# The last convolution: who makes which taps (ScalarE two of 31 for six blocks, VectorE 192 and TensorE 64 tokens of the shared block)

## The chip, the core and the metric

The kernel runs on one NeuronCore of a Trainium2 chip, as one program. The metric is the device time of one execution in microseconds; the median of three runs stands for the kernel. TensorE, VectorE, ScalarE, GpSimd and SyncE each work through their own instructions in the written order and meet at semaphores.

## The reference

The function is a decoder block (gated delta rule with a short convolution, cross attention over a memory, a product-key mixture of experts) followed by two residual mixers over 256 tokens and 1024 channels, all in float32. The change concerns the first of the two, a gated convolution of width 31 along the tokens, one filter for each channel:

```python
def _conv_mixer(h, w_in, dw, db, ln_g, ln_b, w_out):
    a, b, g = jnp.split(h @ w_in, 3, axis=-1)
    y = a * jax.nn.sigmoid(b)
    y = lax.conv_general_dilated(
        y, dw[:, None, :].astype(y.dtype), window_strides=(1,),
        padding=[(CONV_WIDTH_2 // 2, CONV_WIDTH_2 // 2)],
        dimension_numbers=('NWC', 'WIO', 'NWC'),
        feature_group_count=BRANCH) + db
    y = jax.nn.silu(_layernorm(y, ln_g, ln_b)) * jax.nn.silu(g)
    return y @ w_out
```

The second mixer means over windows of 2 to 16 tokens and follows on the result.

## The kernel before, in words

Channels lie on the 128 partitions, in 8 blocks of 128 channels; tokens lie along the free axis. Weights come in units of 1024 x 512 through a ring of three slots, loaded by SyncE.

Most of the time up to 955 us goes to the experts: GpSimd gathers rows, VectorE makes dot products, TensorE adds up weighted rows. The last stage, from about 960 us on, is the two mixers. It is staged in this order on TensorE (function `last_half` makes half a unit, 2 blocks of 256 tokens, 16 products over k of 128x128 by 128x256):

1. `cv_ab0` to `cv_ab3`: eight halves, one for each block k, with `a` of the block in the first 256 columns of a PSUM bank and `b` in the other 256. The halves go round four banks (`last_free`).
2. `cv_g0` and the first half of `cv_g1`: the gate.
3. The convolution of block 7 (256 tokens) and of part of block 6 through diagonal weights: for each tap a 128x128 matrix `tap_diag` with the tap's weights on the diagonal, times the shifted input (line 892).
4. The channel sum "mean" by a matrix of ones over the eight convolved blocks `yc`, in the order 0 to 5, 7, 6 (line 904). It waits for each block by `conv_dve` or `conv_pe`.
5. The second half of `cv_g1`, its first 16 products, then the channel sum "var" of the squares (line 448), then its other 16 products.
6. `cv_out0`, `cv_out1`, and the second mixer.

ScalarE makes `sigmoid(b)` of each block into one of two buffers (`gate_sigmoid(k)`, line 1287, waits for the half on TensorE and for the gated input k-2), and between them the 62 diagonal matrices, 31 for block 7 and then 31 for block 6 (line 1306). The sigmoids 2, 3 and 4 stand in the first loop behind the taps 3, 13 and 23, sigmoid 5 behind that loop, and 6 and 7 in the second loop behind the taps 3 and 13. Then come the Silu of three gate halves (line 1292), which give their banks free, the bias additions of block 7 and of the last 128 tokens of block 6, and the statistics of the layer norm.

VectorE makes the gated input of each block into the padded buffer `ypad` (function `glu`, line 1888, which frees the PSUM bank), and the taps of blocks 0 to 5 on 256 tokens and of block 6 on its first 128 (function `conv_taps`, lines 1900 for tap 0, 1902 for tap 1 and 1905 for the other 29, each multiplying and adding). Even taps gather in `yc`, odd taps in `odd_taps`, and a last addition joins them (line 1908) and posts `conv_dve`. The order is written out: gated input 0, taps 0 to 15 of block 0, gated input 1, taps 16 to 30 of block 0, gated input 2, taps 0 to 15 of block 1 and so on to gated input 7 in the middle of block 3; then blocks 4, 5 and 6 at a stretch. A tap waits for the one two before it, as both write the same buffer.

`go` posts a semaphore and has its own engine wait for it; `post` only posts. In `need(engine, name, n)` the engine waits until the semaphore has reached n.

Of the kernel before, what the change touches and what calls it, by code (L numbers as in the profile page):

```python
# [7 lines left out]
ALU = mybir.AluOpType  # L8
# [3 lines left out]
P = 128  # L12
# [72 lines left out]
for _i, _n in enumerate([f"{u}{g}" for u in ("c", "h", "z") for g in range(4)]):  # L85
    FILLS[1].setdefault(FILL_FROM - 1 + _i, []).append((_n[:-1], int(_n[-1])))
FILLED = [{s + 1: [u for u, g in f if g == 3] for s, f in FILLS[t].items()} for t in range(TT)]

MOD_CHUNKS = 24
# [60 lines left out]
def build(nc, x_t, mem_t, cols_d, c_d, const_d, small_d, keys_d, units_d, grp_d, mod_d, uv_d, out_d, dbg=None):  # L150
    with ExitStack() as ctx:
# [39 lines left out]
        def area(first, n):  # L191
            return arena[:, first:first + n]
# [85 lines left out]
        sgb = blocks(area(2304, 512), 2)  # L278
        odd_taps = area(2816, S)
        tap_diag = [area(a, CV_TAPS * P).rearrange("p (a c) -> p a c", a=CV_TAPS) for a in (M4, 14336)]  # L280
# [154 lines left out]
        def _(pe):  # L435
# [450 lines left out]

            for i, (b, first, n) in enumerate(((7, 0, S), (6, P, P))):
                need(pe, "tap_diag", CV_TAPS * (i + 1))
                need(pe, "glu", b + 1)
                out = tile_begin("ss_m1")[:, 0:n] if i else ps[:, 7, 0:n]  # L890
                for tap in range(CV_TAPS):
                    mm = pe.matmul(out, lhsT=tap_diag[i][:, tap, :], rhs=ypad[:, b, first + tap:first + tap + n],  # L892
                                   start=(tap == 0), stop=(tap == CV_TAPS - 1))
                post(mm, "conv_sums")
# [37 lines left out]
        def _(act):  # L932
            def go(ins, name):
                return did(act, ins, name)
# [367 lines left out]
            gate_sigmoid(0)  # L1302
            gate_sigmoid(1)
            for i, b in enumerate((7, 6)):
                for tap in range(CV_TAPS):
                    post(act.activation(tap_diag[i][:, tap], ident, ACT.Copy, scale=col("cv_dw", 8 * tap + b)), "tap_diag")
                    if tap % 10 == 3 and 2 + 4 * i + tap // 10 < KB:
                        gate_sigmoid(2 + 4 * i + tap // 10)
                if i == 0:
                    gate_sigmoid(5)  # L1310
            for i in range(3):
                gate_silu("cv_g0", i)
            act.wait_ge(sem("conv_sums"), 1)
            go(act.activation(yc[:, 7], ps[:, 7, 0:S], ACT.Identity, bias=col("cv_db", 7)), "conv_pe")
            act.wait_ge(sem("conv_sums"), 2)
            go(act.activation(yc[:, 6, P:S], tile_ps("ss_m1")[:, 0:P], ACT.Identity, bias=col("cv_db", 6)), "conv_pe")
            tile_ready(act, "mean")
# [34 lines left out]
        def _(dve):  # L1352
# [538 lines left out]
            def conv_taps(b, first=0, end=CV_TAPS):  # L1891

                last = counts.get("tap", 0)
                n = P if b == 6 else S
                for tap in range(first, end):
                    w = col("cv_dw", 8 * tap + b)
                    x = ypad[:, b, tap:tap + n]
                    acc = odd_taps[:, 0:n] if tap % 2 else yc[:, b, 0:n]
                    if tap == 0:
                        last = post(V.tensor_scalar(acc, x, w, col("cv_db", b), ALU.mult, ALU.add), "tap")  # L1900
                    elif tap == 1:
                        last = post(V.tensor_scalar(acc, x, w, None, ALU.mult), "tap")
                    else:
                        need(dve, "tap", last - 1)
                        last = post(V.scalar_tensor_tensor(out=acc, in0=x, scalar=w, in1=acc, op0=ALU.mult, op1=ALU.add), "tap")  # L1905
                if end == CV_TAPS:
                    need(dve, "tap", last)
                    go(V.tensor_tensor(yc[:, b, 0:n], yc[:, b, 0:n], odd_taps[:, 0:n], ALU.add), "conv_dve")

# [160 lines left out]
```

## Time and profile before

| | us |
|---|---|
| Median of 3 runs | 1202.87 (1200.65 to 1203.58) |
| The profiled execution | 1203.55 |
| Its span, first to last instruction | 1201.7 |
| TensorE busy | 881.5 (73%) |
| VectorE busy | 814.8 (68%) |
| ScalarE busy | 265.6 (22%) |
| GpSimd busy | 328.3 (27%) |
| Mean granted TensorE clock, of full speed | 0.801 |

Times count from the start of the span. PE is TensorE's matmul and PEld its weight load, DVE VectorE, ACT ScalarE, POOL GpSimd, SP SyncE; L892 is line 892 of the kernel. A float32 matmul of the program stands as two records. A line of the timeline holds instructions of one kind that follow on each other, with their count behind "x"; in square brackets stands the idle time of the engine before them and what ended it. A line of a stretch reads: from:to and length, then for PE, PEld, DVE, ACT and POOL the busy time and, in brackets, how many instructions, then the granted clock (1.00 is 2.4 GHz, 0.50 is 1.2 GHz), the share of the DMA engines, and GB/s; where it is asked for one line of the kernel, only engines that this line uses stand there. Busy shares are means over stages with different limits, so the stretch around the convolution is read by itself.

### The profile page before, as it was taken

The page shows a single profiled execution, that of the slowest core. Times are in us where ns is not written, and L with a number is a line of the kernel's source. Part 1 is how long each engine was busy: PE and PEld are TensorE (multiplying, and loading weights), DVE is VectorE, ACT ScalarE, POOL GpSimd, SP SyncE. Part 2 cuts the span into 40 slices and gives each one's busy share as a digit, 9 for nine tenths or more (in the row PEclk, how much of TensorE's full clock was granted, in tenths as well). Part 3 has the DMA queues.
Part 4 walks back from the last instruction along what each step waited for, and adds up shares of the span by engine and source line. Part 5 has one row for each costly group of instructions (what it writes and reads, how often), then busy time and mean ns, then how long its engine had stood idle before and what let it go on. Part 6 is the DMA issues. An engine that isn't in the chain of part 4 may idle for free.

```text
span 1201.7 us, 17348 instructions
## 1 busy us (share of the span) xinstructions
PE 881.5 (73%) x6784; PEld 668.7 (56%) x6784; DVE 814.8 (68%) x2102; ACT 265.6 (22%) x541; POOL 328.3 (27%) x284
## 2 busy tenths in 40 slices
PE   6999999977786884877344544443445599999998
PEld 6898687865674672754121221211212298878887
DVE  4766546688998767767797687777764779952411
ACT  2511111135222224121021221111102234132100
POOL 0001000242353333534544355454444200000000
PEclk9999899987897896987555655555655599999999
DMA  9987696799999999999999999999999945213330
GB/s 357 395 332 303 232 402 220 308 423 422 388 418 422 411 422 421 420 420 413 420 420 420 402 375 421 420 420 420 420 420 395 371 165 192 96 70 140 106 140 35
DMA packets 51553, 402.49 MB, mean 335 GB/s; under 512 B 5648, under 2 KB 7952, under 8 KB 9104
## 3 DMA queue, kind: packets, MB, share of 16 engines
q0 software_dynamic: 40320, 293.62, 59.8%
q1 hardware_dynamic: 10288, 105.62, 22.1%
q10 hardware_dynamic: 864, 2.16, 0.5%
q8 instruction: 53, 0.87, 0.3%
q14 instruction: 28, 0.23, 0.0%
HBM read 400.32 MB, written 1.05 MB: 334 GB/s over the span
## 4 chain that ended last, share of the span: by engine, by line
PE 22%; DMA 16%; DVE 7%; issue 2%; POOL 2%; ACT 1%; POOLq 0%; DVEq 0%; ACTq 0%
DMA wring<-uv_dram,arena 16%; PE ps L865 15%; PE ps L572 2%; DVE wring L1486 2%; PE ps L892 2%; POOL wring L430 2%; DVE arena L1486 2%; PE ps L559 1%; DVE arena L1513 1%; PE ps L845 1%; PE ps L448 1%; PE ps L923 1%; DVE arena L1427 0%; ACT arena L1331 0%; PE ps L538 0%
## 5 line engine op out<-in xcount | busy, mean ns | idle before, releaser
L430 POOL DMA_INDIRECT arena<-uv_dram,arena x192 | 234.6, 1222 | 339.3 <-PE ps L572 266.8
L572 PE MATMUL ps<-arena 128*32 128x256 f32 x1536 | 160.0, 556 | 220.5 <-DVE arena L1513 220.5
L1486 DVE CUSTOM_DVE_ANT_0 arena<-arena 128x1024 f32<-128x1024 f32 x192 | 231.6, 1224 | 79.5 <-DMA arena<-uv_dram,arena 74.9
L572 PEld LDWEIGHTS ps<-arena 128*32 128x32 f32 x1536 | 52.1, 142 | 309.9 <-DVE arena L1513 261.6
L865 PE MATMUL ps<-xn,wring 128*128 128x256 f32 x608 | 132.0, 379 | 2.4 <-ACT xn L1279 2.4
L865 PEld LDWEIGHTS ps<-xn,wring 128*128 128x128 f32 x608 | 115.4, 190 | 18.3 <-issue 2.7
L1024 ACT ACTIVATE gel<-dots 128x2 f32<-128x2 f32 x128 | 26.0, 203 | 415.2 <-DVE dots L1486 385.6
L484 PEld LDWEIGHTS ps<-xn,wring 128*128 128x128 f32 x896 | 106.2, 198 | 8.5 <-issue 5.9
L484 PE MATMUL ps<-xn,wring 128*128 128x128 f32 x896 | 109.5, 283 | 1.7 <-DVE xn L1527 1.6
L430 POOL DMA_INDIRECT wring<-uv_dram,arena x64 | 80.5, 1258 | 94.5 <-PE ps L572 84.5
L572 PE MATMUL ps<-wring,arena 128*32 128x256 f32 x512 | 52.4, 548 | 69.4 <-DVE arena L1513 69.3
L1486 DVE CUSTOM_DVE_ANT_0 wring<-wring,arena 128x1024 f32<-128x1024 f32 x64 | 77.4, 1223 | 25.0 <-DMA wring<-uv_dram,arena 24.7
L1513 DVE TENSOR_SCALAR arena<-const,gel,arena 128x32 f32<-128x32 f32 x256 | 65.3, 307 | 39.2 <-ACT gel L1024 36.2
L1905 DVE SCALAR_TENSOR_TENSOR arena<-arena,cols 128x256 f32<-128x256 f32 (+1 forms) x203 | 77.4, 460 | 0.6
L572 PEld LDWEIGHTS ps<-wring,arena 128*32 128x32 f32 x512 | 16.8, 140 | 97.6 <-DVE arena L1513 88.8
L484 PE MATMUL ps<-arena,wring 128*128 128x128 f32 x576 | 69.5, 282 | 2.1 <-DVE arena L1739 2.1
L484 PEld LDWEIGHTS ps<-arena,wring 128*128 128x128 f32 x576 | 67.6, 197 | 6.0 <-issue 3.6
L422 POOL DMA_DIRECT2D arena<-mod_dram x24 | 12.9, 539 | 177.8 <-DVE modc L1821 143.6
L1821 DVE CUSTOM_DVE_ANT_0 arena<-arena 128x1024 f32<-128x1024 f32 x48 | 56.8, 1223 | 3.8 <-DMA arena<-mod_dram 1.7
L865 PE MATMUL ps<-arena,wring 128*128 128x256 f32 x256 | 56.8, 382 | 1.6 <-DVE arena L1933 1.6
L865 PEld LDWEIGHTS ps<-arena,wring 128*128 128x128 f32 x256 | 48.1, 190 | 10.2 <-DVE arena L1933 2.6
L512 PE MATMUL ps<-xn,wring 128*128 128x128 f32 x384 | 51.3, 294 | 0.0
(267 smaller groups left out, 1160.3 us busy)
## 6 DMA issues: line engine op xcount, KB each, us to landing
wring<-units_dram SPq DMA_DIRECT2D x46, 2048.0 KB, 11.4
arena<-mod_dram POOLq DMA_DIRECT2D x24, 1024.0 KB, 9.5
arena<-uv_dram,arena POOLq DMA_INDIRECT x192, 13.8
wring<-units_dram SPq DMA_DIRECT2D x2, 1024.0 KB, 8.4
arena<-units_dram SPq DMA_DIRECT2D x1, 2048.0 KB, 8.8
hA<-x_t_dram SPq DMA_DIRECT2D x2, 512.0 KB, 7.1
arena<-mem_t_dram SPq DMA_DIRECT2D x1, 1024.0 KB, 9.8
arena<-keys_dram ACTq DMA_DIRECT2D x2, 512.0 KB, 6.8
```

Of the source, the lines that this page charges most:

```text
L422: pool.dma_start(mod_w[:, i % MOD_BUFFERS].rearrange("p b d -> p (b d)"), mod_d[i]).then_inc(sem(f"mod_in{i % MOD_BUFFERS}"), 16)
L430: pool.indirect_dma_start(ring[b], None, uv_d, bass.IndirectOffsetOnAxis(ap=idx[:, n:n + 1], axis=0)).then_inc(sem(f"row_in{b}"), 16)
L484: mm = pe.matmul(out[:, j * P:(j + 1) * P], lhsT=lhsT, rhs=src[:, k, :], start=(k == 0), stop=(k == KB - 1))
L512: mm = pe.matmul(out[:, g * P:(g + 1) * P], lhsT=w[:, k, g * P:(g + 1) * P], rhs=xn[:, k, tokens(t)], start=(k == 0), stop=(k == KB - 1))
L572: mm = pe.matmul(acc_ps(q)[G * c:G * (c + 1), :], lhsT=diag[:, s % 2, j, :], rhs=ring[b][:, D + 256 * c:D + 256 * (c + 1)], start=(p == 0 ...
L865: mm = pe.matmul(out[:, j * S:(j + 1) * S], lhsT=w[:, k, (2 * i + j) * P:(2 * i + j + 1) * P], rhs=rhs[:, k, :], start=(k == 0), stop=(k = ...
L892: mm = pe.matmul(out, lhsT=tap_diag[i][:, tap, :], rhs=ypad[:, b, first + tap:first + tap + n], start=(tap == 0), stop=(tap == CV_TAPS - 1))
L1024: post(act.activation(gel[:, s % 2], dots[:, s % 2], ACT.Gelu), "gelu")
L1486: post(V.tensor_tensor_reduce(out=ring[b][:, 0:D], in0=ring[b][:, 0:D], in1=x_rep[q % 2], scale=1.0, scalar=0.0, op0=ALU.mult, op1=ALU.add ...
L1513: post(V.tensor_scalar(diag[:, s % 2, j], cst("stack"), gel[:, s % 2, j:j + 1], gate[:, n:n + 1], ALU.mult, ALU.mult), "diag")
L1821: post(V.tensor_tensor_reduce(out=w, in0=w, in1=silu_c, scale=1.0, scalar=0.0, op0=ALU.mult, op1=ALU.add, accum_out=modc[:, m:m + 1]), "mo ...
L1905: last = post(V.scalar_tensor_tensor(out=acc, in0=x, scalar=w, in1=acc, op0=ALU.mult, op1=ALU.add), "tap")
```

## The change

Six edits. A constant `CV_SPLIT` of 192 takes the place of 128 as the number of tokens of block 6 that VectorE makes; TensorE makes the other 64 and ScalarE adds the bias to these. There are two buffers `odd_taps`, for even and odd blocks. ScalarE has a function `first_taps(b)`, which for blocks 1 to 6 makes tap 0 (with the bias) into `yc` and tap 1 into the block's `odd_taps` and then posts `first_taps`. It is called for block 1 behind sigmoid 3 and for block 2 behind sigmoid 4 in the first loop of diagonals, and for blocks 3 to 6 behind the second loop, ahead of the Silus of the gate. From block 3 on it waits until VectorE has finished block b - 2. VectorE leaves out taps 0 and 1 of these blocks and waits for `first_taps` in their place; taps 2 and 3 no longer wait for a tap before them.

```diff
--- before.py
+++ after.py
@@ -85,6 +85,9 @@
 for _i, _n in enumerate([f"{u}{g}" for u in ("c", "h", "z") for g in range(4)]):
     FILLS[1].setdefault(FILL_FROM - 1 + _i, []).append((_n[:-1], int(_n[-1])))
 FILLED = [{s + 1: [u for u, g in f if g == 3] for s, f in FILLS[t].items()} for t in range(TT)]
+
+
+CV_SPLIT = 192
 
 MOD_CHUNKS = 24
 MOD_BUFFERS = 4
@@ -276,7 +279,7 @@
         hB = blocks(area(12288, 2048), KB)
         ypad = area(0, 8 * 286).rearrange("p (b t) -> p b t", b=KB)
         sgb = blocks(area(2304, 512), 2)
-        odd_taps = area(2816, S)
+        odd_taps = [area(2816 + S * i, S) for i in range(2)]
         tap_diag = [area(a, CV_TAPS * P).rearrange("p (a c) -> p a c", a=CV_TAPS) for a in (M4, 14336)]
         yc, gT, ycn = (blocks(area(5120 + 2048 * i, 2048), KB) for i in range(3))
         vpad = area(14336, 8 * 272).rearrange("p (b t) -> p b t", b=KB)
@@ -884,7 +887,7 @@
             last_half("cv_g1", 0, xn)
 
 
-            for i, (b, first, n) in enumerate(((7, 0, S), (6, P, P))):
+            for i, (b, first, n) in enumerate(((7, 0, S), (6, CV_SPLIT, S - CV_SPLIT))):
                 need(pe, "tap_diag", CV_TAPS * (i + 1))
                 need(pe, "glu", b + 1)
                 out = tile_begin("ss_m1")[:, 0:n] if i else ps[:, 7, 0:n]
@@ -1301,19 +1304,33 @@
             go(act.activation(warm[:], cst("one"), ACT.Sigmoid), "warm")
             gate_sigmoid(0)
             gate_sigmoid(1)
+
+            def first_taps(b):
+
+                n = CV_SPLIT if b == 6 else S
+                need(act, "glu", b + 1)
+                if b >= 3:
+                    need(act, "conv_dve", b - 1)
+                act.activation(yc[:, b, 0:n], ypad[:, b, 0:n], ACT.Identity, bias=col("cv_db", b), scale=col("cv_dw", b))
+                go(act.activation(odd_taps[b % 2][:, 0:n], ypad[:, b, 1:1 + n], ACT.Copy, scale=col("cv_dw", 8 + b)), "first_taps")
+
             for i, b in enumerate((7, 6)):
                 for tap in range(CV_TAPS):
                     post(act.activation(tap_diag[i][:, tap], ident, ACT.Copy, scale=col("cv_dw", 8 * tap + b)), "tap_diag")
                     if tap % 10 == 3 and 2 + 4 * i + tap // 10 < KB:
                         gate_sigmoid(2 + 4 * i + tap // 10)
+                        if i == 0 and tap > 3:
+                            first_taps(tap // 10)
                 if i == 0:
                     gate_sigmoid(5)
+            for b in range(3, KB - 1):
+                first_taps(b)
             for i in range(3):
                 gate_silu("cv_g0", i)
             act.wait_ge(sem("conv_sums"), 1)
             go(act.activation(yc[:, 7], ps[:, 7, 0:S], ACT.Identity, bias=col("cv_db", 7)), "conv_pe")
             act.wait_ge(sem("conv_sums"), 2)
-            go(act.activation(yc[:, 6, P:S], tile_ps("ss_m1")[:, 0:P], ACT.Identity, bias=col("cv_db", 6)), "conv_pe")
+            go(act.activation(yc[:, 6, CV_SPLIT:S], tile_ps("ss_m1")[:, 0:S - CV_SPLIT], ACT.Identity, bias=col("cv_db", 6)), "conv_pe")
             tile_ready(act, "mean")
             tile_used_wait(act, act.activation(rms[:, 0], tile_ps("mean")[:, 0:S], ACT.Copy, scale=1.0 / D), "mean")
             signal(act, "mean_sb", 1)
@@ -1891,21 +1908,24 @@
             def conv_taps(b, first=0, end=CV_TAPS):
 
                 last = counts.get("tap", 0)
-                n = P if b == 6 else S
+                n = CV_SPLIT if b == 6 else S
                 for tap in range(first, end):
                     w = col("cv_dw", 8 * tap + b)
                     x = ypad[:, b, tap:tap + n]
-                    acc = odd_taps[:, 0:n] if tap % 2 else yc[:, b, 0:n]
-                    if tap == 0:
+                    acc = odd_taps[b % 2][:, 0:n] if tap % 2 else yc[:, b, 0:n]
+                    if tap < 2 and b:
+                        need(dve, "first_taps", b)
+                    elif tap == 0:
                         last = post(V.tensor_scalar(acc, x, w, col("cv_db", b), ALU.mult, ALU.add), "tap")
                     elif tap == 1:
                         last = post(V.tensor_scalar(acc, x, w, None, ALU.mult), "tap")
                     else:
-                        need(dve, "tap", last - 1)
+                        if b == 0 or tap > 3:
+                            need(dve, "tap", last - 1)
                         last = post(V.scalar_tensor_tensor(out=acc, in0=x, scalar=w, in1=acc, op0=ALU.mult, op1=ALU.add), "tap")
                 if end == CV_TAPS:
                     need(dve, "tap", last)
-                    go(V.tensor_tensor(yc[:, b, 0:n], yc[:, b, 0:n], odd_taps[:, 0:n], ALU.add), "conv_dve")
+                    go(V.tensor_tensor(yc[:, b, 0:n], yc[:, b, 0:n], odd_taps[b % 2][:, 0:n], ALU.add), "conv_dve")
 
 
             go(V.memset(ypad[:, :, 0:15], 0.0))
```

## Rows read from the trace of the kernel before

**Rows 1.** The page: lines of the chain that ended last, shares of span.
```profile
DMA wring<-uv_dram,arena 16%; PE ps L865 15%; PE ps L572 2%; DVE wring L1486 2%; PE ps L892 2%; POOL wring L430 2%; DVE arena L1486 2%; PE ps L559 1%; DVE arena L1513 1%; PE ps L845 1%; PE ps L448 1%; PE ps L923 1%; DVE arena L1427 0%; ACT 
```

**Rows 2.** The chain in order of time from 1000 us: start, length, what.
```profile
1000.00 37.34 PE ps L865 x173
1037.34 20.31 PE ps L892 x124
1057.64 3.46 PE ps L904 x16
1061.10 3.45 PE ps L865 x16
1064.55 3.47 PE ps L448 x16
```

**Rows 3.** Timeline, 982 to 1065 us: start, length, engine, line, operation.
```profile
982.79 0.42 DVE L1888 TENSOR_TENSOR arena<-ps,arena 128x256 f32<-128x256 f32 x1
...
983.96 5.62 DVE L1905 SCALAR_TENSOR_TENSOR arena<-arena,cols 128x256 f32<-128x256 f32 x14
...
989.03 0.38 ACT L1287 ACTIVATE arena<-ps 128x256 f32<-128x256 f32 x1 [3.46 <-PE ps L865]
...
989.50 0.42 DVE L1888 TENSOR_TENSOR arena<-ps,arena 128x256 f32<-128x256 f32 x1
990.06 6.03 DVE L1905 SCALAR_TENSOR_TENSOR arena<-arena,cols 128x256 f32<-128x256 f32 x15
...
996.12 0.43 DVE L1908 TENSOR_TENSOR arena<-arena 128x256 f32<-128x256 f32 x1
...
1016.65 0.38 ACT L1287 ACTIVATE arena<-ps 128x256 f32<-128x256 f32 x1 [3.46 <-PE ps L865]
1017.07 5.07 ACT L1306 ACTIVATE arena<-const,cols 128x128 f32<-128x128 f32 x17
...
1036.84 0.41 DVE L1900 TENSOR_SCALAR arena<-arena,cols 128x256 f32<-128x256 f32 x1
...
1037.43 11.57 DVE L1905 SCALAR_TENSOR_TENSOR arena<-arena,cols 128x256 f32<-128x256 f32 x29
1049.04 0.42 DVE L1908 TENSOR_TENSOR arena<-arena 128x256 f32<-128x256 f32 x1
1049.50 0.34 DVE L1900 TENSOR_SCALAR arena<-arena,cols 128x128 f32<-128x128 f32 x1
...
1049.95 7.70 DVE L1905 SCALAR_TENSOR_TENSOR arena<-arena,cols 128x128 f32<-128x128 f32 x29
...
1057.68 0.29 DVE L1908 TENSOR_TENSOR arena<-arena 128x128 f32<-128x128 f32 x1
...
1062.98 2.19 ACT L1323 ACTIVATE arena<-arena 128x512 f32<-128x512 f32 x4
```

**Rows 4.** Groups by form, ScalarE, from 1000 us: busy us, mean ns.
```profile
L1306 ACT ACTIVATE arena<-const,cols 128x128 f32<-128x128 f32 x31 | 9.4, 387 | 0.1
...
L1331 ACT ACTIVATE arena<-arena,cols 128x256 f32<-128x256 f32 x8 | 4.8, 600 | 0.3
```

**Rows 5.** Stretches, matmuls of line 892, then of line 624: busy, clock.
```profile
1050.90:1057.30 6.40, 6.40 (x60) 6.40 (x59) 1.00 0.00 0
...
18.90:20.40 1.50, 1.50 (x15) 1.50 (x15) 1.00 1.23 415
```

**Rows 6.** Stretches, all engines: busy (count) per engine, TensorE's granted clock.
```profile
919.90:921.90 2.00, 0.00 (x0) 0.00 (x0) 0.00 (x0) 1.96 (x3) 0.00 (x0) 1.00 0.99 414
921.90:924.00 2.10, 0.00 (x0) 0.00 (x0) 0.24 (x2) 1.77 (x3) 0.00 (x0) 0.50 1.02 425
958.60:962.80 4.20, 4.18 (x19) 4.18 (x20) 2.98 (x10) 2.55 (x6) 0.00 (x0) 0.50 1.03 437
962.90:967.50 4.60, 4.60 (x43) 4.60 (x43) 0.00 (x0) 0.00 (x0) 0.00 (x0) 1.00 0.93 395
```

## The prediction

> **What bounds the kernel now.** I read the page's chain of waits first, then the same chain in order of time for the last 200 us, then the timeline of that stretch engine by engine, and last single stretches for the granted clock. The reader is to see in [rows 1] that next to a transfer the largest part of the chain is TensorE at line 865, the projections of the last stage, and in [rows 2] that the last fifth hangs on TensorE: from 1000 us to 1068 us its matmuls follow one another without a hole, first the projections, then the two convolutions through diagonal weights (line 892), the channel sum "mean" (line 904), half of cv_g1 (line 865) and the sum "var" (line 448). But VectorE is hardly behind. [Rows 3] show its taps: from the gated input of block 2 at 982.79 to the last addition of block 6, which ends at 1057.68 + 0.29 = 1057.97, it goes from one instruction to the next with no wait of note. TensorE leaves the second convolution at some 1057.6 and ends "mean" at 1061.10 [rows 2]. Block 6 is its last term: two records at a step of 0.216 (sixteen in 3.46) and the rest of the last one, 0.6 us in all, so its input may come up to 1060.5, while it comes at 1057.97. VectorE has 2.5 us of slack; what moves its end beyond 1060.5 moves the kernel's end.
>
> **ScalarE's taps.** For blocks 1 to 6 the first two taps leave VectorE, where they cost 0.59 us of its time per block (1037.43 less 1036.84) and 0.45 us at 128 tokens (1049.95 less 1049.50) [rows 3]. On ScalarE a 128x256 ACTIVATE with scale and bias from columns takes 0.60 us, and a 128x128 one with scale alone 0.387 [rows 4]. The second one of a pair is 128x256 with scale alone, so between these, and I take 0.49. 17 copies of 128x128 span 5.07 [rows 3], a step of 0.293, so back-to-back ones overlap by 0.09. A pair is 0.60 - 0.09 + 0.49 = 1.00 us. ScalarE is idle for most of this stretch and its own time costs nothing. What counts is when the pair comes, because VectorE now waits for it before its third tap.
>
> ScalarE works in the written order, and two of the pairs stand behind things that come late:
> - Block 1: its pair is behind the sigmoid of block 3, which follows TensorE at 989.03 and takes 0.38 [rows 3]. The pair starts at 989.44, ends at 990.44, VectorE goes on at 990.49. Before, it began tap 2 at 983.96: 6.5 us of wait. Queued behind it on VectorE are the gated input 3 and all other blocks.
> - From there by the steps of [rows 3] (14 taps and on to the gated input 5.54, then 0.56, 15 taps 6.06, an addition 0.46): gated input 3 at 996.0, addition 1002.7, gated input 4 at 1003.1. TensorE's halves come every 6.9 us (four from 989.03 to 1016.65), and the bank of block 3 is next wanted for block 7, after 1009.7: it is free in time.
> - Block 2: its pair is behind the sigmoid of block 4 (989.03 + 6.9 = 995.9), done at 997.3, before VectorE asks. Taps begin at 1003.7; gated input 5 at 1009.2; addition 1015.8; gated input 6 at 1016.3, VectorE ready for block 3 at 1016.9.
> - Block 3: its pair stands behind the whole second loop of diagonals, in which the sigmoid of block 7 follows TensorE at 1016.65 and then 17 diagonal copies run from 1017.07 to 1022.14 [rows 3]. The pair starts at 1022.16 and ends at 1023.16; VectorE begins tap 2 at 1023.2, after 6.3 us of wait. The first wait is swallowed by this one, whose end TensorE sets.
> - Then: gated input 7 at 1028.75 (TensorE's convolution wants it at 1037.3: safe), addition of block 3 at 1035.4, tap 2 of block 4 at 1035.8. The pair of block 4 needs only the end of block 2 and is there. Block 5's waits for the end of block 3 (1035.8) and has all of block 4 as cover; block 6's for the end of block 4, covered by block 5. A full block is 11.61 + 0.46 = 12.07: addition of block 4 at 1047.4, of block 5 at 1059.5, tap 2 of block 6 at 1059.97 (before 1049.95: 10.0 late).
>
> The three Silu evictions of cv_g0 and their table load now stand behind the pair of block 6: from about 1049 to 1052, not spread from 1022 on. Their banks and results are wanted after "var"; the bias addition of block 7 moves to 1052.5 and is wanted at 1060. "Mean" with its wait for VectorE hides both, and without it each microsecond would count. No DMA is moved. The dropped waits before taps 2 and 3 give nothing: taps follow at 0.400 (11.61/29) by their own length.
>
> **64 more tokens on VectorE.** A tap step is 0.400 at 256 tokens and 0.2666 at 128 (1057.68 less 1049.95, by 29) [rows 3]. No row has 192, so 29 taps take between 7.73 and 11.61, and I take the middle, 9.67, as the two are most likely points of one line. The final addition becomes 0.36. Block 6 ends at 1059.97 + 9.67 + 0.36 = 1070.0, against 1057.97: 12.0 late.
>
> **64 fewer tokens on TensorE.** The second convolution makes 62 records of 128 columns (each tap two). 60 of them begin in 6.40 us, 0.107 each, and the weight loads beside them fill the stretch; with weights of the same 128x128 and only 8 columns, line 624 begins 15 in 1.50 us, 0.100 and at the window's edge 0.107, at the same clock [rows 5]. 64 columns lie between 8 and 128, and so the gain between 0 and 0.4 us; if the step went with the columns it would be half of 6.6, 3.3 us. I take 0, by line 624. The convolution ends long before VectorE either way.
> The Trainium skill (TensorE: Matmul & The Clock Gate, Back-to-back issue gap) gives the spacing of an isolated matmul as N/2.4 + 2.5 ns, 29 ns at 64 columns, which makes an estimate of 1.8 us for 62 of them; its section LDWEIGHTS (loading the stationary operand) gives a weight load by its columns alone, P/1.2, 107 ns at 128. By the second nothing is gained, and the trace agrees with it, 0.107. By the first this sum would be the same too, since VectorE comes last, but the rival without a wait would gain.
>
> **What follows on TensorE.** It works off "mean" for blocks 0 to 5 (the last from 1059.9) and 7 and stands idle from some 1060.9 to 1070.05: nine microseconds with nothing that it may do, as the half of cv_g1 stands behind "mean". What the clock does in such a hole: from 919.9 on TensorE does nothing, the grant is still 1.00 up to 921.9 and 0.50 after (1.2 GHz in place of 2.4); and when it took up full work at 958.6, the grant stayed at 0.50 to 962.8 and was 1.00 from 962.9 [rows 6]. I take both: half speed from 1070.05 for 4.2 us, to 1074.25.
> - The two records of block 6 for "mean": 0.43 each, so the half of cv_g1 begins at 1070.9.
> - Of its 16 records 7.8 fit before 1074.25 at 0.43; the other 8.2 at 0.216 take 1.8: end at 1076.0. At full clock the sixteen take 3.45 (1061.10 to 1064.55, [rows 2]).
> - "Var" needs the squares. The first is done at 1062.98 + 0.62 [rows 3], 2.5 after "mean", the last at 1065.2, 4.1 after; so now at 1073.6 to 1075.2, before TensorE asks. It begins at 1076.1 where it did at 1064.5: 11.6 late.
> Behind "var" the order is as it was and so are the waits, up to the output.
>
> **Sum.** +12.0 for VectorE's end, less 2.5 of slack, gives 9.5; plus 2.1 for the clock +11.6. The profiled execution took 1203.55 us, with a span of 1201.7; it becomes 1215.15. It is 0.68 above the median of the runs, 1202.87, so the forecast is **1214.5 us**. The unknown sizes: the taps at 192 tokens plus or minus 1.9 at their ends, the clock from 0 (1212.4) to 5 (1217.4).
>
> **Rivals.**
> - *The clock stays up.* At 919.9 the grant outlived the end of the work by 2 us [rows 6], and a shorter hole would pass. This one is four times that, which speaks against. Then +9.5, 1212.4.
> - *The clock comes back late*, so that "var" runs at half speed too: 3 us more, 1217.5. For it: the grant has been 0.50 where work is thin. Against: here it is dense, as from 958.6 on.
> - *Only block 1 waits,* because ScalarE has the pair of block 3 when VectorE comes. The steps above less the second wait (6.3): VectorE's end is 1063.7, 3.2 after 1060.5, 1206.1. Against it is the written order: the sigmoid that follows 1016.65 and 17 copies stand in front.
> - *No wait decides, the faster side.* If ScalarE is always ahead, VectorE loses 5 x 0.59 + 0.45 and gains 1.94 + 0.07: 1.4 earlier, 1056.6. With the second convolution bound by its weights TensorE leaves it as before and the time is 1202.9. Only if 64 columns take half the step does it reach "mean" 3.3 earlier, at 1054.3, and then the last term ends at 1056.6 + 0.6 = 1057.2, 3.9 earlier, 1199.0. The gain begins where both hold, ScalarE's pair of block 3 before 1017 and a step below 0.107; the order contradicts the first, line 624 the second.
>
> **Numbers.** The forecast 0.72, clock stays 0.14, clock late 0.07, block 1 alone 0.03, no wait at 1202.9 0.02, no wait and half a step 0.02. A difference of 0.3% (3.6 us) is about what a measurement of this kernel can tell. Range 1211.0 to 1217.3: it takes in the clock that stays, with taps somewhat below the middle, and the edge of the late one. Faster 0.02; same 0.03, the 0.02 and some of "block 1 alone"; slower 0.95.
>
> **What would show it.** VectorE idle twice for some 6 us, released by ScalarE, behind 984 and behind 1017; its final addition of block 6 near 1069.6; TensorE's records of the second convolution still at 0.107; its hole of 9 us before 1070, a grant of 0.50 behind it and the half of cv_g1 taking 5.1 in place of 3.45; all from "var" on in the same shape, shifted. I am wrong if VectorE's taps run on over 984 and 1017, or if these holes are there and the end moves by under 8 us.

## The result, and the profile after

The changed kernel takes 1215.92 us in the median of four runs (1212.57 to 1221.73), the kernel before 1202.65 in four: the ratio is 1.0113, with a 95% interval of 1.0086 to 1.0140, slower by 13.3 us. The profiled execution took 1217.19 us with a span of 1215.3.

The timeline of the changed kernel has the lines that answer to [rows 3]: start and length in us, engine, line, operation, in brackets the idle time ahead and what ended it. Lines 1314 and 1315 are ScalarE's pair, 1925 VectorE's taps, 1928 its last addition, 895 and 907 TensorE's convolution and channel sum, 868 the gate (like all projections), 451 the sum of squares. Line numbers are those of each kernel's own file, so they shift between variants. A matmul of the program stands as two records. A gate half is 16 matmuls; "the 16 records of the gate" below are the 8 of them that stand between the channel sum and the sum of squares, and the other 8 follow behind that sum.

```profile
990.32 0.38 ACT L1290 ACTIVATE arena<-ps 128x256 f32<-128x256 f32 x1 [3.46 <-PE ps L868]
...
990.74 0.60 ACT L1314 ACTIVATE arena<-arena,cols 128x256 f32<-128x256 f32 x1
991.24 0.49 ACT L1315 ACTIVATE arena<-arena,cols 128x256 f32<-128x256 f32 x1
...
991.84 5.63 DVE L1925 SCALAR_TENSOR_TENSOR arena<-arena,cols 128x256 f32<-128x256 f32 x14 [7.34 <-ACT arena L1315]
...
1018.36 5.07 ACT L1319 ACTIVATE arena<-const,cols 128x128 f32<-128x128 f32 x17
1023.34 0.58 ACT L1314 ACTIVATE arena<-arena,cols 128x256 f32<-128x256 f32 x1
1023.83 0.49 ACT L1315 ACTIVATE arena<-arena,cols 128x256 f32<-128x256 f32 x1
...
1024.43 5.63 DVE L1925 SCALAR_TENSOR_TENSOR arena<-arena,cols 128x256 f32<-128x256 f32 x14 [6.25 <-ACT arena L1315]
...
1061.19 9.64 DVE L1925 SCALAR_TENSOR_TENSOR arena<-arena,cols 128x192 f32<-128x192 f32 x29
...
1070.86 0.36 DVE L1928 TENSOR_TENSOR arena<-arena 128x192 f32<-128x192 f32 x1
...
1071.28 1.22 PE L907 MATMUL ps<-arena,const 128*128 128x256 f32 x2 [8.93 <-DVE arena L1928]
...
1072.29 5.60 PE L868 MATMUL ps<-xn,wring 128*128 128x256 f32 x16
1072.60 0.38 ACT L1335 ACTIVATE arena<-ps 128x256 f32<-128x256 f32 x1 [13.30 <-PE ps L907]
```

Where [rows 2] had one piece of TensorE after another from 1000 to 1068, the chain in order of time now leaves TensorE at 1017.92 and goes over ScalarE's diagonals and its pair to VectorE, and comes back at 1071.28:

```profile
999.99 17.93 PE ps L868 x83
...
1020.71 2.72 ACT arena L1319 x9
1023.43 0.49 ACT arena L1314
1023.93 0.41 ACT arena L1315
...
1071.28 1.22 PE ps L907 x2
1072.50 5.39 PE ps L868 x16
1077.89 3.47 PE ps L451 x16
```

Stretches of the changed kernel (busy time per engine in the order PE, PEld, DVE, ACT, POOL, then the granted clock) show what the hole did, as [rows 6] do for the expert stage; the reader is to see the grant fall while TensorE is idle and come back between 1076 and 1077, at about 1076.3, some 5.0 us after work was taken up at 1071.28:

```profile
1062.00:1064.00 2.00, 0.34 (x2) 0.00 (x0) 2.00 (x7) 0.00 (x0) 0.00 (x0) 1.00 0.03 8
1064.00:1070.00 6.00, 0.00 (x0) 0.00 (x0) 6.00 (x19) 0.00 (x0) 0.00 (x0) 0.67 0.00 0
...
1075.00:1076.00 1.00, 1.00 (x4) 0.82 (x3) 0.63 (x2) 1.00 (x4) 0.00 (x0) 0.50 0.00 0
1076.00:1077.00 1.00, 1.00 (x5) 0.83 (x5) 0.00 (x0) 0.57 (x2) 0.00 (x0) 0.85 0.00 0
1077.00:1078.00 1.00, 1.00 (x7) 0.87 (x6) 0.00 (x0) 0.00 (x0) 0.00 (x0) 1.00 0.00 0
```

The expert stage ahead of the change ends at times that scatter from one execution to the next: the first sigmoid starts between 963.8 and 972.0 us in the profiles of this study. So all times in the table are counted from that first sigmoid, "s" in short (968.37 in the kernel before, 969.65 in the changed one). Each figure is a start or an end in that kernel's timeline less s; "read" is the start of the ScalarE instruction that reads the sum, and the last column is the end of VectorE's last instruction. Each row is one profiled execution:

| us from s | VectorE's end of block 6 | channel sum read | squares' sum read | second mixer's sum read | last instruction of VectorE |
|---|---|---|---|---|---|
| before | 89.60 | 92.83 | 99.74 | 137.25 | 230.58 |
| changed | 101.57 | 102.95 | 111.79 | 149.30 | 242.90 |
| changed, again | 101.57 | 102.94 | 112.19 | 149.69 | 244.78 |
| pair 1 early | 101.57 | 102.94 | 111.91 | 149.42 | 242.74 |
| pair 3 early | 95.53 | 96.38 | 103.29 | 140.79 | 234.39 |
| all pairs early | 89.95 | 92.84 | 99.74 | 137.25 | 230.57 |
| the same, inputs later | 88.20 | 92.84 | 99.74 | 137.25 | 230.57 |
| hole filled | 101.57 | 102.42 | 109.32 | 146.83 | 240.43 |
| 192 tokens alone | 91.65 | 92.84 | 99.75 | 137.26 | 230.58 |
| changed, 128 tokens | 99.57 | 100.95 | 109.45 | 146.96 | 240.56 |
| built from the theory | 90.17 | 91.03 | 97.39 | 135.93 | 230.92 |
| fillers spread | 90.21 | 91.06 | 97.42 | 134.93 | 229.94 |
| second hole filled | 90.19 | 91.05 | 97.41 | 134.93 | 228.25 |

From the second mixer's sum to the end it takes 93.3 us in the kernel before and in five variants, but 93.6 in the changed kernel and in "pair 3 early", "hole filled" and "128 tokens": the hole of TensorE behind that sum is 2.63 or 2.64 us long there, not 2.36. No run explains this 0.27 us. The three rows with 95.0 or 95.1 are those in which the clock fell at this hole (see below).

### The profile page after: what moved, and what is told of

Its sections match the earlier page's. It is cut to its first block and busy times, and to the rows that moved or that the text cites. A ratio compares the mean times of both kernels' runs of the same rounds, so it can differ in the third digit from the quotient of the medians.

```text
span 1215.3 us, 17361 instructions
## 1 busy us (share of the span) xinstructions
PE 895.0 (74%) x6784; PEld 675.8 (56%) x6784; DVE 813.3 (67%) x2090; ACT 271.5 (22%) x553; POOL 329.7 (27%) x284
## 5 line engine op out<-in xcount | busy, mean ns | idle before, releaser
L575 PE MATMUL ps<-arena 128*32 128x256 f32 x1536 | 163.4, 567 | 214.9 <-DVE arena L1530 214.9
L868 PEld LDWEIGHTS ps<-xn,wring 128*128 128x128 f32 x608 | 116.9, 193 | 19.3 <-issue 3.0
L487 PE MATMUL ps<-xn,wring 128*128 128x128 f32 x896 | 111.4, 286 | 3.4 <-DMA wring<-units_dram 1.8
L487 PEld LDWEIGHTS ps<-xn,wring 128*128 128x128 f32 x896 | 107.9, 201 | 10.5 <-issue 6.1
L575 PE MATMUL ps<-wring,arena 128*32 128x256 f32 x512 | 55.2, 573 | 64.8 <-DVE arena L1530 64.8
L1925 DVE SCALAR_TENSOR_TENSOR arena<-arena,cols 128x256 f32<-128x256 f32 (+1 forms) x203 | 79.4, 469 | 14.5 <-ACT arena L1315 13.6
L515 PEld LDWEIGHTS ps<-xn,wring 128*128 128x128 f32 x384 | 50.4, 214 | 5.7 <-issue 5.7
```

The costliest lines, as they stand in the source:

```text
L487: mm = pe.matmul(out[:, j * P:(j + 1) * P], lhsT=lhsT, rhs=src[:, k, :], start=(k == 0), stop=(k == KB - 1))
L515: mm = pe.matmul(out[:, g * P:(g + 1) * P], lhsT=w[:, k, g * P:(g + 1) * P], rhs=xn[:, k, tokens(t)], start=(k == 0), stop=(k == KB - 1))
L575: mm = pe.matmul(acc_ps(q)[G * c:G * (c + 1), :], lhsT=diag[:, s % 2, j, :], rhs=ring[b][:, D + 256 * c:D + 256 * (c + 1)], start=(p == 0 ...
L868: mm = pe.matmul(out[:, j * S:(j + 1) * S], lhsT=w[:, k, (2 * i + j) * P:(2 * i + j + 1) * P], rhs=rhs[:, k, :], start=(k == 0), stop=(k = ...
```

## The experiments

The theory is that of the forecast: VectorE waits for ScalarE's pair of block 3, whose place in ScalarE's queue ties it to sigmoid 7 and 17 diagonals; this makes VectorE 12 us late, and TensorE's hole then costs more by its clock. The rivals are that the waits add up, that the 192 tokens or ScalarE's work beside VectorE cost the time, and that the clock had no part. Ratios are to the kernel before as it was timed beside the variants: 1203.03 us for the changed kernel again, pair 1 early, pair 3 early and hole filled; 1202.56 for all pairs early, 192 tokens alone, 128 tokens and built from the theory; 1203.90 for the other three.

**The changed kernel again.**

> The changed kernel once more, as the measure for the three variants timed beside it. Expected 13 us over the kernel before, 10 to 16, with VectorE idle 7.3 us before block 1 and 6.3 us before block 3, TensorE idle 8.9 us before the last term of the channel sum, and a granted clock of 0.50 for 4 to 5 us behind that.

1218.39 us, ratio 1.0126 (1.0090 to 1.0162). Up to the channel sum it repeats to 0.01 us. The sum of squares is read 0.40 later, as the grant stays at 0.50 for some 5.8 us behind the hole in place of 5.0. And from the second mixer's sum read to the end it takes 95.1 us, 1.5 more than the 93.6 of the first execution. The stretches say why: ahead of the second mixer's first unit TensorE has a hole of 2.64 us (2.63 in the first execution; the kernel before has one of 2.36 there, and its grant stays), and in this execution the grant fell at its end. The first line is the kernel before, the others are this execution.

```profile
1107.88 55.49 PE L865 MATMUL ps<-xn,wring 128*128 128x256 f32 x256 [2.36 <-ACT xn L1279]
```

```profile
1120.10:1122.70 2.60, 0.04 (x1) 0.00 (x0) 1.43 (x4) 1.46 (x4) 0.00 (x0) 0.94 0.99 422
1122.80:1125.40 2.60, 2.60 (x6) 2.14 (x7) 1.73 (x5) 2.60 (x7) 0.00 (x0) 0.50 0.14 60
1125.90:1130.00 4.10, 4.10 (x21) 3.61 (x20) 0.00 (x0) 0.00 (x0) 0.00 (x0) 1.00 0.00 0
```

**Pair 1 early.** ScalarE's loop makes it ahead of sigmoid 2:

```diff
+                        if i == 0 and tap == 3:
+                            first_taps(1)
                         gate_sigmoid(2 + 4 * i + tap // 10)
-                        if i == 0 and tap > 3:
-                            first_taps(tap // 10)
+                        if i == 0 and tap == 23:
+                            first_taps(2)
```

> The changed kernel with ScalarE's pair of block 1 moved ahead of sigmoid 2. Theory (the wait for block 3 ends at a time that TensorE and the diagonals set, and swallows the wait for block 1): VectorE no longer idles before block 1, but idles some 13 us before block 3 and begins its taps at the same time as in the changed kernel, 0.0 to 0.2 us different in the stage; time as the changed kernel, 13 us over before. Rival (the waits add): 6 us less than the changed kernel.

1214.37 us, ratio 1.0095 (1.0062 to 1.0128), an interval that overlaps that of the changed kernel. The trace is sharper: VectorE's first wait of 7.34 is gone, the second has grown from 6.25 to 12.37, and block 6 ends at 101.57 as before. The first wait was swallowed to the last 0.01 us. VectorE's line for block 3 in this kernel's timeline:

```profile
1021.81 1.28 DVE L1927 SCALAR_TENSOR_TENSOR arena<-arena,cols 128x256 f32<-128x256 f32 x3 [12.37 <-ACT arena L1315]
```

**Pair 3 early.**

```diff
                     gate_sigmoid(5)
-            for b in range(3, KB - 1):
+                    first_taps(3)
+            for b in range(4, KB - 1):
                 first_taps(b)
```

> The changed kernel with the pair of block 3 moved behind sigmoid 5; block 1 still waits. Theory: VectorE idles only once, 7.3 us before block 1, makes up 0.59 us in each block, and ends block 6 5.7 us later than before, 3.2 after the point from which TensorE waits: before + 3.2 us, with a TensorE hole of 2 to 3 us and a clock that stays at 1.00 (with a fall: before + 5.3). Rival (the extra time lies in the 192 tokens or in ScalarE's work beside VectorE, not in the wait): no more than 2 us less than the changed kernel, that is before + 10 or more.

1207.84 us in ten runs, ratio 1.0041 (1.0015 to 1.0067). Block 6 ends 5.93 us later than before (expected 5.7), the squares' sum is read 3.55 later (expected 3.2), 8.5 to 8.9 earlier than in the two executions of the changed kernel. One call moved ahead in ScalarE's queue takes back some seven tenths of the loss (8.5 of 12.05). TensorE's hole is 3.28 us here, and the 16 records of the gate still take their 3.45. TensorE's timeline first, then stretches of all engines; the reader is to see the grant at 1.00 through the hole and behind it:

```profile
1066.11 0.70 PE L907 MATMUL ps<-arena,const 128*128 128x256 f32 x2 [3.28 <-DVE arena L1929]
1066.65 3.62 PE L868 MATMUL ps<-xn,wring 128*128 128x256 f32 x16
1070.10 3.62 PE L451 MATMUL ps<-arena,const 128*128 128x256 f32 x16
```

```profile
1064.00:1065.00 1.00, 0.00 (x0) 0.00 (x0) 1.00 (x5) 0.00 (x0) 0.00 (x0) 1.00 0.00 0
1065.00:1066.00 1.00, 0.00 (x0) 0.00 (x0) 0.97 (x4) 0.00 (x0) 0.00 (x0) 1.00 0.00 0
...
1068.00:1070.00 2.00, 2.00 (x11) 1.77 (x10) 1.94 (x4) 1.99 (x4) 0.00 (x0) 1.00 0.00 0
```

**All pairs early.** Pair 1 stands ahead of sigmoid 2 as in the first variant, and the others so (the pair of block 2, now early, also waits until block 0 is done with their common buffer):

```diff
-                if b >= 3:
+                if b >= 2:
                     need(act, "conv_dve", b - 1)
...
+                        if (i, tap) == (0, 13):
+                            first_taps(2)
+                        if (i, tap) == (1, 13):
+                            first_taps(4)
                 if i == 0:
                     gate_sigmoid(5)
-            for b in range(3, KB - 1):
+                    first_taps(3)
+            for b in range(5, KB - 1):
                 first_taps(b)
```

> The changed kernel with every pair where VectorE need not wait for it: block 1 ahead of sigmoid 2, block 2 behind sigmoid 3, block 3 behind sigmoid 5, block 4 behind sigmoid 7. Theory: the forecast's rival without a wait took VectorE's end as 1.4 us earlier than before; but gated input 7 can't come before sigmoid 7, whose time TensorE sets and which VectorE met before within 0.1 us, so what is saved in blocks 1 to 3 is waited away there and only 1.6 us are left against 2.0 for the 64 tokens: VectorE ends 0.2 to 0.5 us later than before, TensorE's sums begin as before: before +0.0, within 1 us. If the forecast's sum holds, VectorE ends 1.4 earlier, and the time is the same. If 64 columns made the second convolution cheaper, it would leave 3.3 us earlier and the time be 2 us less than before.

1203.92 us in twelve runs, ratio 1.0018 (1.0002 to 1.0033); in the stage it is the kernel before, 0.00 at the squares' sum and 0.01 at the end. The ratio lies 0.02% outside 1 all the same; the profiles show no cause for that in this stage, and with the inputs later (below) it is 0.9995. With the waits gone all of the loss is gone, tokens and ScalarE's twelve ACTIVATEs and all. VectorE ends 0.35 later than before, not 1.4 earlier. It now meets the sigmoids: gated inputs 3, 5 and 7 wait 0.39, 0.45 and 0.44 for sigmoids whose times TensorE's halves set. The last one:

```profile
1016.36 0.38 ACT L1290 ACTIVATE arena<-ps 128x256 f32<-128x256 f32 x1 [3.46 <-PE ps L868]
1016.77 0.42 DVE L1910 TENSOR_TENSOR arena<-ps,arena 128x256 f32<-128x256 f32 x1 [0.44 <-ACT arena L1290]
```

**The same, inputs later.** Gated inputs 2 to 7 come 4 to 10 taps later in VectorE's order, as none of the taps that now go first needs them (beside this, one of two equal waits for `first_taps` goes):

```diff
-            for b in range(4):
+            for b in range(1, 4):
+                conv_taps(b, 0, 4 + 2 * b)
                 glu(2 * b)
-                conv_taps(b, 0, 16)
+                conv_taps(b, 4 + 2 * b, 20 + 2 * b)
                 glu(2 * b + 1)
-                conv_taps(b, 16)
+                conv_taps(b, 20 + 2 * b)
```

> The variant with all pairs early (192 tokens on VectorE), with gated inputs 2 to 7 set 4 to 10 taps later on VectorE. Theory: VectorE's waits for the sigmoids (0.4 to 0.5 us, three of them, where it had been paced by TensorE) are gone, and it ends block 6 1.4 us earlier than in the kernel before, 88.2 us from the first sigmoid in place of 89.6, which is the sum of the forecast's rival; the sum of squares and the end don't move (TensorE sets them): before within 1 us. Rival (ScalarE's pairs slow VectorE, or its steps don't add up): 89.0 or later.

1202.49 us, ratio 0.9995 (0.9973 to 1.0018). VectorE ends at 88.20, 1.40 earlier than before and just the forecast's sum for a VectorE that does not wait; nothing behind it moves, since TensorE's two sums start as before.

**Hole filled.** 19 matmuls whose results nothing reads stand in TensorE's hole:

```diff
-                else:
+                elif k < 6:
                     need(pe, "conv_dve", k + 1)
                 if k == 6:
                     need(pe, "conv_pe", 2)
+                    need(pe, "conv_dve", 6)
+                    spare_bank = tile_begin("var")
+                    for i in range(19):
+                        pe.matmul(spare_bank[:, 0:S], lhsT=ones, rhs=yc[:, 0, :], start=True, stop=True)
+                    need(pe, "conv_dve", 7)
```

> The changed kernel with 19 matmuls of ones by block 0 put in TensorE's hole, between the term of block 7 and that of block 6 of the channel sum, into the bank of the sum behind it, which is overwritten later: 38 records, 8.2 us, of a hole of 8.9 us. Their results are not used. Theory (the hole lets the clock fall, which costs 2.7 us behind it): the grant stays at 1.00, the last term and the 16 records of the gate half take 0.43 + 3.45 us, and the sum of squares begins 2.7 us earlier than in the changed kernel, before + 10.4. Rival (the squares or the table load of ScalarE are what the sum of squares waits for, whatever the clock): less than 1 us.

1212.59 us, ratio 1.0088 (1.0056 to 1.0120). VectorE's end is the same 101.57, the squares' sum is read at 109.32 in place of 111.79 and 112.19: 2.5 to 2.9 less, where 2.7 was expected. With these matmuls the grant is 1.00 throughout, and the 16 records of the gate take their old 3.45.

```profile
1058.30 8.36 PE L910 MATMUL ps<-arena,const 128*128 128x256 f32 x38
1067.39 0.70 PE L912 MATMUL ps<-arena,const 128*128 128x256 f32 x2 [0.73 <-DVE arena L1933]
1067.93 3.62 PE L868 MATMUL ps<-xn,wring 128*128 128x256 f32 x16
1071.38 3.62 PE L451 MATMUL ps<-arena,const 128*128 128x256 f32 x16
```

```profile
1058.00:1067.00 9.00, 8.66 (x41) 7.28 (x39) 8.96 (x29) 0.00 (x0) 0.00 (x0) 1.00 0.01 2
1067.00:1075.00 8.00, 7.61 (x35) 6.73 (x36) 2.83 (x5) 3.86 (x6) 0.00 (x0) 1.00 0.00 0
```

**192 tokens alone,** on the kernel before:

```diff
-            for i, (b, first, n) in enumerate(((7, 0, S), (6, P, P))):
+            for i, (b, first, n) in enumerate(((7, 0, S), (6, 192, S - 192))):
...
-                n = P if b == 6 else S
+                n = 192 if b == 6 else S
```

> The kernel before with 192 tokens of block 6 on VectorE and 64 on TensorE, nothing else changed. Theory: VectorE's block 6 takes 9.67 + 0.36 us in place of 7.73 + 0.29 and ends at 1060.0, within the slack that ends at 1060.5; the 62 records of TensorE still take 0.107 each: before +0.0, within 1 us. Rival (TensorE's step goes with the columns): its convolution ends 3.3 us earlier, and the channel sum then waits for VectorE.

1202.80 us in twelve runs, ratio 0.9996 (0.9979 to 1.0014). VectorE ends 2.05 later and TensorE does not notice, as the end lies within its slack. TensorE's convolution is not shorter at 64 columns: the bias addition of block 7 starts at 1050.30 and that of block 6 at 1057.23, 6.93 apart, where the kernel before has 1050.76 and 1057.75, 6.99 apart. From 1051 to 1056 us 47 of its records begin in 5.00 us, 0.107 each as with 128 columns. The first two lines are the kernel before, the others this variant.

```profile
1050.76 0.47 ACT L1314 ACTIVATE arena<-ps,cols 128x256 f32<-128x256 f32 x1 [12.79 <-PE ps L892]
1057.75 0.37 ACT L1316 ACTIVATE arena<-ps,cols 128x128 f32<-128x128 f32 x1 [6.51 <-PE ps L892]
```

```profile
1049.52 9.63 DVE L1905 SCALAR_TENSOR_TENSOR arena<-arena,cols 128x192 f32<-128x192 f32 x29
1050.30 0.47 ACT L1314 ACTIVATE arena<-ps,cols 128x256 f32<-128x256 f32 x1 [12.79 <-PE ps L892]
...
1057.23 0.32 ACT L1316 ACTIVATE arena<-ps,cols 128x64 f32<-128x64 f32 x1 [6.46 <-PE ps L892]
1059.19 0.36 DVE L1908 TENSOR_TENSOR arena<-arena 128x192 f32<-128x192 f32 x1
```

**The changed kernel with 128 tokens.**

```diff
-CV_SPLIT = 192
+CV_SPLIT = 128
```

> The changed kernel with 128 tokens of block 6 on VectorE again. Theory: VectorE is the one that comes last, so the end moves by what block 6 loses, 1.9 to 2.1 us: 2 us less than the changed kernel, before + 11. Rival (TensorE's longer records matter): no gain.

1213.05 us, ratio 1.0084 (1.0060 to 1.0109). VectorE ends 2.00 earlier, the squares' sum is read 2.3 to 2.7 earlier than in the two executions of the changed kernel. What was free within the slack costs its full size once VectorE is last: the channel sum is read 2.0 earlier. The rest is the clock, which came back 4.3 us after the hole (6.93 us long here) in place of 5.0 and 5.8.

**Built from the theory.** VectorE makes all 256 tokens of block 6 and TensorE none, so ScalarE's 31 diagonals and the bias addition for it go too; the pairs are early (block 4's only behind the last sigmoid, like those of 5 and 6) and the inputs late as above; of the gate half 11 matmuls stand ahead of the last term of the channel sum and 5 behind it:

```diff
-CV_SPLIT = 192
+CV_SPLIT = 256
...
+            for k in (0, 1, 2, 3, 4, 5, 7):
+                mean_term(k)
...
+            for j in range(2):
+                for k in range(KB):
+                    if (j, k) == (1, 3):
+                        post(mean_term(6), "tiles")
+                    mm = pe.matmul(out[:, j * S:(j + 1) * S], lhsT=w[:, k, (2 + j) * P:(3 + j) * P],
+                                   rhs=xn[:, k, :], start=(k == 0), stop=(k == KB - 1))
+            post(mm, "last_pairs")
+            sum_channels("var", sq_all, S, squared(0))
```

> A version built from the theory: TensorE makes none of block 6 (62 records, 6.6 us, and 31 diagonal copies less), VectorE all 256 tokens, ScalarE's pairs early as in the variant before, gated inputs 2 to 7 set 4 to 10 taps later on VectorE so that it never waits for a sigmoid, and the gate half of TensorE put around the last term of the channel sum: 11 of its 16 matmuls ahead of it, 5 behind it, then the sum of squares. Theory: VectorE ends block 6 at 1058.6 (0.6 later than before), the channel sum ends at 1059.3 in place of 1061.1, the sum of squares ends 2 to 3 us earlier than before: before - 2.5, between -1.5 and -3.5. Rival (ScalarE's statistics between the two sums set the pace): between -1.5 and 0.

1201.44 us in twelve runs, ratio 0.9986 (0.9968 to 1.0004), not told apart from the kernel before. The squares' sum is read 2.35 us earlier, as expected. But the expected 2.5 us at the end did not come: at the second mixer's sum 1.32 is left, and the end is 0.34 later. The last 16 records of the gate, which stood behind the squares' sum before, had covered the way through layer norm and Silu to `cv_out0`. Now TensorE waits there 4.38 us and the grant falls; it falls once more at the later hole of 2.36, whose unit takes 1.7 us longer.

```profile
1070.09 12.15 PE L868 MATMUL ps<-arena,wring 128*128 128x256 f32 x42 [4.38 <-DVE arena L1974]
```

```profile
1067.43:1068.43 1.00, 0.00 (x0) 0.00 (x0) 1.00 (x4) 1.00 (x1) 0.00 (x0) 1.00 0.58 246
1068.43:1069.43 1.00, 0.00 (x0) 0.00 (x0) 1.00 (x4) 0.95 (x3) 0.00 (x0) 0.80 0.08 33
...
1074.43:1075.43 1.00, 1.00 (x4) 0.76 (x3) 0.42 (x1) 0.00 (x0) 0.00 (x0) 0.50 0.00 0
1075.43:1076.43 1.00, 1.00 (x5) 0.86 (x4) 0.00 (x0) 0.00 (x0) 0.00 (x0) 0.78 0.00 0
```

**Fillers spread.** Of the gate's 16 matmuls 7 stand ahead of the last term of the channel sum, 3 between it and the sum of squares and 6 behind that; the diff is against the version before:

```diff
-                    if (j, k) == (1, 3):
+                    if (j, k) == (0, 7):
                         post(mean_term(6), "tiles")
+                    if (j, k) == (1, 2):
+                        sum_channels("var", sq_all, S, squared(0))
...
-            sum_channels("var", sq_all, S, squared(0))
```

> The version built from the theory, with the 16 matmuls of the gate half spread over TensorE's three holes: 7 ahead of the last term of the channel sum, 3 between it and the sum of squares, 6 behind the sum of squares (in the version before all 16 stood ahead of the sum of squares, and the hole of 4.4 us behind it let the clock fall to 0.50 for some 6 us). Theory: no hole is over 2 us, the grant stays at 1.00 there, the sum of squares is read at 97.4 us from the first sigmoid as in the version before (99.74 in the kernel before), and cv_out0 follows at the distance it has in the kernel before, so the end comes 2.3 us earlier in the stage: before - 2.3, or - 0.7 where the clock falls in the later hole of 2.6 us as it did there. Rival (the gain of the first sum is lost behind it whatever TensorE does): before - 0.5 to 0.

1203.77 us in twelve runs, ratio 0.9998 (0.9978 to 1.0017). In the stage the gain of the squares' sum now reaches the second mixer's sum whole (134.93 against 137.25, 2.32), as the holes are 1.86, 1.37 and 1.79 and the unit behind them starts at its old distance. In the profiled execution 1.7 of it is lost at the later hole of 2.36: the grant fell about 0.9 us after TensorE had taken up work again at 1107.97.

```profile
1108.00:1109.00 1.00, 1.00 (x5) 0.89 (x6) 1.00 (x4) 1.00 (x4) 0.00 (x0) 0.96 0.77 328
1109.00:1111.00 2.00, 2.00 (x6) 1.57 (x5) 0.99 (x3) 1.62 (x5) 0.00 (x0) 0.50 0.02 8
```

**Second hole filled.**

```diff
             sum_channels("ss_m1", sq_all, S, squared(1))
+            spare_bank = tile_begin("mean")
+            need(pe, "mean_sb", 1)
+            for i in range(5):
+                pe.matmul(spare_bank[:, 0:S], lhsT=ones, rhs=ycn[:, 0, :], start=True, stop=True)
```

> The same, with five matmuls of no use in the hole between the last sum of squares and the second mixer's first unit (2.2 us of 2.4 to 2.6), into a bank that nothing reads any more. Theory: the clock can't fall there, which it did in one of two executions of the changed kernel and in the version before, at 1.5 us each: from the last sum of squares read to the end 93.3 us, and in the mean over runs up to 1 us less than the variant without. Rival (the fall there is rare): the same time as that variant.

1200.83 us in twelve runs, ratio 0.9978 (0.9957 to 0.9999) to the kernel before: the only version whose interval lies below 1, and that by 0.01%, which is thin for one of several versions. In the stage it is 2.33 us faster (228.25 against 230.58), and the hole is 0.20 with the grant at 1.00. It beats the variant without the five matmuls by 2.9 us in the median, 1200.83 against 1203.77. That is more than a fall of the clock in every execution would give (1.7), and the expert stage ahead scatters by 8 us between profiles, so the two medians don't measure this effect. What the traces show is that the grant fell at this hole in three of the twelve profiles in which it is open (the second of the changed kernel and the two versions before this one), at 1.5 to 1.7 us each, and not in the one in which it is filled; that one profile can't show that filling prevents it.

```profile
1106.67 2.32 PE L931 MATMUL ps<-arena,const 128*128 128x256 f32 x10
1109.19 21.17 PE L868 MATMUL ps<-xn,wring 128*128 128x256 f32 x97 [0.20 <-ACT xn L1300]
```

## Why the prediction was right, by its steps

- **VectorE's two waits.** Forecast 6.5 and 6.3 us behind tap 2's old times, released by ScalarE. Measured as idle time 7.34 and 6.25; the first includes the 0.75 us that lay between the gated input and tap 2 before, so that tap 2 of block 1 comes 6.6 later (22.19 from s against 983.96 less 968.37). Right, and the first is swallowed: pair 1 early moves nothing.
- **The pair.** Forecast 1.00 us from 0.60 and 0.49; measured 0.50 to the second one's start and 0.49, so 0.99. Right.
- **192 tokens.** Forecast 9.67 and 0.36 from the middle of two sizes; measured 9.64 and 0.36. Alone they cost nothing, behind the waits they cost 2.0 us at the channel sum.
- **VectorE's end.** Forecast 12.0 later; 101.57 less 89.60 is 11.97.
- **The slack.** Forecast 2.5. The channel sum is read 0.85 us after VectorE's end wherever that comes last and the clock is up (pair 3 early, hole filled), and 3.23 after it in the kernel before: the slack was 2.38.
- **64 columns on TensorE.** Forecast no gain. The two bias additions are 6.93 apart where they were 6.99. The bound by the 8-column row of [rows 5] held.
- **The clock.** Forecast a fall in the hole and 4.2 us at half speed behind it, 2.1 us lost. It was 5.0 us at half speed, 5.8 in the second execution and 5.3 with pair 1 early, and the loss is 2.5, 2.9 and 2.6 against the kernel with the hole filled. The mechanism is right; the length of this stretch is the term that was mis-sized, by 0.4 to 0.8 us of time.
- **The sum.** Forecast +11.6 at the squares' sum; measured 12.05 (11.97 less 2.38, plus 2.5 for the clock) and 12.45. The end is 12.3 later in the first execution, with the unexplained 0.27; in the second it is 14.2 later, of which 1.5 is a second fall of the clock, in a hole that the forecast had passed over. The medians differ by 13.3. The profiled executions differ by 13.6, 12.3 in this stage and 1.3 ahead of it, where the expert stage ended 1.28 later. Some luck is in how near 1214.5 and 1215.92 are: timed again, the same kernel had a median of 1218.39, above the forecast's upper end of 1217.3.
- **The rival without a wait** was mis-sized in a step: it took all that VectorE saves as VectorE's gain, 1.4. The kernel with all pairs early has VectorE 0.35 later, because in blocks 1 to 3 its gated inputs 3, 5 and 7 already started within 0.1 us of the ends of sigmoids that TensorE paces (989.50 behind 989.41, for one). With the inputs set later it is 1.40 earlier. For the time neither matters: 0.0 in both, as the forecast had said for a convolution bound by its weights.
- **The rival "block 1 alone"** was realized by moving pair 3: forecast +3.2, measured 3.55 at the squares' sum, 3.8 at the end of the stage, and +4.9 us (0.41%) by the ratio, whose interval reaches from 1.8 to 8.1.

## What to carry to other kernels

Work that is moved to an idle engine costs nothing there, but it arrives when that engine's queue comes to it: look at what stands in front of it, and what that waits for, before counting what the busy engine saves. Two waits in a row don't add where the second ends at a time set from outside; moving the first one alone gave nothing here, and moving the second gave 8.5 us. And in a stage where TensorE's order is the bound, a filler matmul is worth what it covers, not its own length: taken from one hole it opens another, and the hole is paid twice where the clock falls in it.

## What the runs showed of the hardware that was not expected

- The same short hole of TensorE is not the same to the clock each time. One of 2.64 us (the changed kernel, second execution) and two of 2.36 (built from the theory, fillers spread) had the grant fall to 0.50 at their end or within 1 us behind it, which cost 1.5 to 1.7 us; one of 3.28 (pair 3 early), one of 2.63 (the changed kernel, first execution) and one of 2.36 (the kernel before) left it at 1.00. The length of the hole alone does not decide.
- With the grant at 0.50 and TensorE busy without a break, the time until it was 1.00 again differed: 5.0, 5.3 and 5.8 us behind the same hole of 8.93 us (changed, pair 1 early, changed again), 4.3 behind one of 6.93 (128 tokens), 4.2 in [rows 6], and some 3 us behind the hole of 2.64 (work from 1122.78 on, 1.00 from 1125.9 on).
- 62 float32 records with 128x128 weights take 6.99 us from one result to the next at 128 columns and 6.93 at 64; a new one begins every 0.107 us at both.
